# Merge-gate blocks of a prompt attention: eight plain filler products a layer become four seven-product pairs, and the fifth pair follows

## The reference

```
h = RMSNorm(x);  P = h @ w_in
A = NSA(P)      compressed, selected and window softmax attention, sigmoid gates
B = GLA(P)      gated linear attention, per-head RMSNorm, swish output gate
x += (sigmoid(gA) * (A @ w_pa) + sigmoid(gB) * (B @ w_pb)) @ w_out
x += (gelu(conv3(h2 @ w_u)) * (h2 @ w_g)) @ w_down,   h2 = RMSNorm(x)
```

## Time and profile before

| what | value |
|---|---|
| median of 3 runs (lowest, highest) | 2190.35 us (2189.44, 2193.3) |
| profiled execution, its own time | 2181.98 us |
| its span | 2180.2 us |
| mean granted TensorE clock | 0.993 of full speed |
| TensorE / VectorE / ScalarE / GpSimd busy | 98% / 51% / 23% / 27% |
| attention units 1 to 31, first layer | 306 to 462 us |

### The profile page before, as it was taken

One profiled execution on the slowest core, in us unless ns is written; L12 is line 12 of the kernel. 1 busy time (PEld: TensorE's weight loads), 2 busy tenths in 40 slices (PEclk: granted clock), 3 DMA queues, 4 the chain that ended last, 5 costly groups with the idle time before them and its releaser, 6 DMA issues.

```text
span 2180.2 us, 30270 instructions
## 1 busy us (share of the span) xinstructions
PE 2130.5 (98%) x12007; PEld 1708.9 (78%) x12007; DVE 1115.2 (51%) x2318; ACT 511.5 (23%) x1100; POOL 585.5 (27%) x565
## 2 busy tenths in 40 slices
PE   8998999999999999999999989999999999999999
PEld 7786866678887888888887867766788878888887
DVE  5566646654345555543326666466544364555522
ACT  3123124432112222210112231343221212222000
POOL 5140010102322444434331400101032224444332
PEclk9999999999999999999999999999999999999999
DMA  6774531112221322222293736311132222222222
GB/s 167 259 250 167 223 126 39 40 42 100 78 81 59 96 78 78 80 78 92 59 293 115 265 136 247 101 36 24 47 114 81 78 70 85 78 78 91 77 77 74
DMA packets 172303, 237.52 MB, mean 109 GB/s; under 512 B 39551, under 2 KB 151680, under 8 KB 169408
## 3 DMA queue, kind: packets, MB, share of 16 engines
q1 hardware_dynamic: 153320, 133.11, 20.3%
q0 software_dynamic: 18400, 102.36, 12.7%
q10 hardware_dynamic: 444, 0.12, 0.0%
HBM read 222.76 MB, written 21.11 MB: 112 GB/s over the span
## 4 chain that ended last, share of the span: by engine, by line
PE 90%; DVE 5%; DMA 2%; ACT 2%; issue 1%; POOL 0%; DVEq 0%; SPq 0%; ACTq 0%; POOLq 0%
PE PS L948 44%; PE PS L891 18%; PE PS L1077 6%; PE PS L913 5%; PE PS L939 3%; PE PS L1411 2%; PE PS L1328 2%; PE PS L1339 2%; DMA arena<-in_cache_kv_slc_dram,idx 2%; PE PS L442 2%; ACT arena L1621 1%; PE PS L1286 1%; DVE arena L2307 1%; PE PS L1311 1%; DVE arena L1997 1%
## 5 line engine op out<-in xcount | busy, mean ns | idle before, releaser
L948 PE MATMUL PS<-arena,ring 128*128 128x272 f32 x1536 | 376.7, 393 | 0.9 <-DVE xT L1991 0.6
L1621 ACT ACTIVATE arena<-PS 128x272 f32<-128x272 f32 (+11 forms) x438 | 175.6, 425 | 770.1 <-PE PS L948 277.8
L891 PE MATMUL PS<-hT,ring 128*128 128x272 f32 x1408 | 338.9, 400 | 3.1 <-DVE small L2473 1.9
L948 PEld LDWEIGHTS PS<-arena,ring 128*128 128x128 f32 x1536 | 291.5, 190 | 61.5 <-issue 1.7
L891 PEld LDWEIGHTS PS<-hT,ring 128*128 128x128 f32 x1408 | 270.0, 194 | 67.4 <-issue 12.2
L1991 DVE TENSOR_TENSOR arena<-PS,arena 128x272 f32<-128x272 f32 (+4 forms) x222 | 106.6, 489 | 327.2 <-PE PS L948 237.3
L1991 DVE TENSOR_TENSOR xT<-PS,xT 128x272 f32<-128x272 f32 x224 | 98.9, 442 | 252.2 <-PE PS L948 252.0
L948 PE MATMUL PS<-hT,ring 128*128 128x272 f32 x832 | 207.6, 393 | 0.1
L948 PEld LDWEIGHTS PS<-hT,ring 128*128 128x128 f32 x832 | 158.3, 191 | 32.9
L1997 DVE SCALAR_TENSOR_TENSOR arena<-arena,prm 128x32 f32<-128x32 f32 (+1 forms) x176 | 142.6, 810 | 22.1 <-ACT arena L1621 18.2
L948 PE MATMUL PS<-arena,kv_kT 128*128 128x272 f32 x616 | 149.7, 392 | 0.0
(11 more groups left out here) (350 smaller groups left out, 2754.2 us busy)
## 6 DMA issues: line engine op xcount, KB each, us to landing
ring<-in_w_up_dram SPq DMA_DIRECT2D x88, 512.0 KB, 4.6
ring<-in_w_in_dram SPq DMA_DIRECT2D x68, 512.0 KB, 4.8
ring<-in_w_down_dram SPq DMA_DIRECT2D x32, 512.0 KB, 4.5
arena<-in_state_kv_win_dram POOLq DMA_DIRECT2D x4, 2048.0 KB, 8.3
ring<-in_w_out_dram SPq DMA_DIRECT2D x16, 512.0 KB, 4.6
out_dram<-in_state_kv_win_dram POOLq DMA_DIRECT2D x2, 4064.0 KB, 39.9
ring<-in_w_down_dram SPq DMA_DIRECT2D x16, 384.0 KB, 3.8
ring<-in_w_in_dram SPq DMA_DIRECT2D x16, 256.0 KB, 4.6
```

What stands on the lines that cost most here:

```text
L891: mm = pe.matmul(PS[0:m, b + a, 0:HALF], weight(k), rhs(k)[:, HALF * a:HALF * a + HALF], start=(k == 0), stop=(k == nk - 1))
L948: mm = pe.matmul(PS[:, bank, 0:HALF], weight[:, k, :], rhs(k), start=(start and k == 0), stop=(stop and k == kc - 1), skip_group_check=not ...
L1621: return nc.scalar.activation(out, in_, func, **kw)
```

## The change

`ma0` to `ma3` become fillers of seven products each (`side_seven`), after units 9, 15, 21 and 28, in place of eight plain fillers after units 8, 11, 14, 17, 20, 23, 26 and 30. They use one pair of banks: each bank is accumulated on after ScalarE has copied, or VectorE has added, what stood in it. `mb0` becomes a `gate_seven`, with the third and fourth head norm between its second and third product. GpSimd makes the token sums before the attention units instead of in unit 22 (the third in three pieces), changes `hT` in place after `rb11`, and makes the weight sums of `ma0` at once, of `ma1` to `ma3` each after the pair before it, and of `mb0` after the sampled updates. ScalarE and VectorE get the copies and additions; counters and buffers are renumbered.

```diff
-    for j, name in zip((2, 5, 8, 11, 14, 17, 20, 23, 26, 30), ["rb10", "rb11"] + [f"ga{m}" for m in range(KC)]):
+    for j, name in zip((2, 5, 9, 15, 21, 28), ["rb10", "rb11"] + SIDED):
...
-                gp.wait_ge(*S.at(gp, "kd_ready", 1))
+                def weight_sums(name):
...
+                    if n >= EARLY + 2:
+                        gp.wait_ge(*S.filled(gp, last_ticket(SEVENS[n - 2])))
+                    elif 1 <= n < EARLY:
+                        gp.wait_ge(*S.filled(gp, last_ticket(SEVENS[n - 1])))
+                    gp.wait_ge(*w_landed(gp, name))
...
-                gp.tensor_tensor(gsum[2], high[:, :, 0:HALF], gsum[1], ALU.subtract).then_inc(*S.inc(gp, "g_sum"))
+                gp.tensor_tensor(gpair, high[:, 0:2, 0:HALF], gsum[1][:, 0:2, :], ALU.subtract).then_inc(*S.inc(gp, "g_sum"))
+                for k in (2, 3):
+                    gp.tensor_tensor(gsum4[k], high[:, k, 0:HALF], gsum[1][:, k, :], ALU.subtract).then_inc(*S.inc(gp, "g_sum"))
+                weight_sums("ma0")
+                gp.wait_ge(*S.filled(gp, "rb11"))
+                gp.tensor_tensor(low[:, :, HALF:NT], high[:, :, HALF:NT], low[:, :, HALF:NT], ALU.subtract).then_inc(*S.inc(gp, "g_sum"))
+                for name in SIDED[1:]:
+                    weight_sums(name)
...
+                gp.wait_ge(*S.filled(gp, "us3"))
+                weight_sums("mb0")
...
+            def side_seven(name, pool):
...
+                half_product(x, quarter(s, 4, 0, 0), lambda k: hT[:, k, 0:HALF], 4, True, True).then_inc(*S.inc(pe, "side_part"))
+                pe.wait_ge(*S.at(pe, "g_sum", 1))
+                pe.wait_ge(*S.at(pe, "w_sum", 4 * n + 1))
+                half_product(z, new[0], lambda k: gsum[0][:, k, :], 4, True, True).then_inc(*S.inc(pe, "side_part"))
+                pe.wait_ge(*S.at(pe, "side_copied", 3 * i + 1))
...
+                half_product(x, new[1], lambda k: gsum[1][:, k, :], 4, False, True).then_inc(*S.inc(pe, "side_part"))
+                pe.wait_ge(*S.at(pe, "side_copied", 3 * i + 2))
+                pe.wait_ge(*S.at(pe, "w_sum", 4 * n + 4))
+                half_product(z, new[2], lambda k: hT[:, 4 + k, HALF:NT], 4, False, True).then_inc(*S.inc(pe, "side_part"))
+                pe.wait_ge(*S.at(pe, "side_copied", 3 * i + 3))
+                pe.wait_ge(*S.at(pe, "g_sum", 6))
+                half_product(x, quarter(s, 4, 0, 1), lambda k: hT[:, k, HALF:NT], 4, False, True).then_inc(*S.inc(pe, "side_part"))
+                pe.wait_ge(*S.at(pe, "side_met", 3 * i + 1))
+                half_product(z, quarter(s, 4, 1, 0), lambda k: hT[:, 4 + k, 0:HALF], 4, True, True).then_inc(*S.inc(pe, "side_part"))
+                pe.wait_ge(*S.at(pe, "side_met", 3 * i + 2))
+                pe.wait_ge(*S.at(pe, "g_sum", 5))
+                half_product(x, quarter(s, 4, 1, 1), lambda k: gsum4[k], 4, False, True).then_inc(*S.fill(pe, name))
...
-                sb_ = wload("mb0")
-                fm("S", "gb0", sb_, 0)
-                out_norm(2)
-                out_norm(3)
-                fm("S", "gb1", sb_, P)
...
+                gate_seven(0, "S", last_norms)
...
-                    ahead = j + 3 if ("u", j - 1) in SIDE_AT else j + 2
+                    before = SIDE_AT.get(("u", j - 1), ("",))[0]
+                    if before in SIDED_AT:
+                        n, m = SIDED_AT[before], 2 * SIDED_AT[before]
+                        if done < min(j + 2, len(units)):
+                            exps(done)
+                            done += 1
+                        side_take(before, 6 * n + 1, 0, gaT[:, m, 0:HALF])
+                        side_take(before, 6 * n + 2, 1, gaT[:, m + 1, HALF:NT])
+                    ahead = j + 3 if before else j + 2
                     while done < min(ahead, len(units)):
                         exps(done)
                         done += 1
+                    if before in SIDED_AT:
+                        side_take(before, 6 * n + 3, 0, gaT[:, m, HALF:NT])
...
+                        if name in SIDED_AT:
...
+                            dv.wait_ge(*S.at(dv, "side_part", 6 * n + 4))
+                            dv.wait_ge(*S.at(dv, "side_copied", 3 * n + 3))
+                            tt(d0[:, HALF:NT], PS[:, b + 1, 0:HALF], d0[:, HALF:NT], ALU.add).then_inc(*S.inc(dv, "side_met"))
+                            dv.wait_ge(*S.at(dv, "side_part", 6 * n + 5))
+                            tt(d1[:, HALF:NT], PS[:, b, 0:HALF], d1[:, HALF:NT], ALU.add).then_inc(*S.inc(dv, "side_met"))
+                            dv.wait_ge(*S.at(dv, "side_part", 6 * n + 6))
+                            tt(d0[:, 0:HALF], PS[:, b + 1, 0:HALF], d0[:, 0:HALF], ALU.add).then_inc(*S.inc(dv, "side_met"))
+                            dv.wait_ge(*S.at(dv, "side_met", 3 * n + 3))
+                            dv.wait_ge(*S.filled(dv, name))
+                            copy(d1[:, 0:HALF], PS[:, b, 0:HALF]).then_inc(*S.drain(dv, name))
...
+                    if h == 1:
+                        add_seven("mb0", "gb0", "gb1", sB[0], sB[1])
```

More of the change, by code:

```diff
@@ L239, in last_ticket @@
         return f"{kind}{2 * i}"
-    if kind == "mb" and i:
+    if kind == "ma":
+        return name
+    if kind == "mb":
         return f"gb{2 * i}"
@@ L498, in quarter, with weight_parts @@
             return ring[:, slot, 0:2 * kc * WCOLS].rearrange("p (k n) -> p k n", n=WCOLS)[:, kc * lower:kc * lower + kc, P * second:P * second + P]
+        def weight_parts(name, kc):
+            n = SEVEN_AT[name]
+            if n >= EARLY:
+                return [sums[(n - EARLY) % 2][:, i, 0:kc, :] for i in range(3)]
+            return early_sums + [late_sum[n // len(SIDED)]]
         def down_pool(n):
@@ L949, in half_product, with seven_products @@
                 return mm
-            def seven_products(name, pool, first, second, kc, top, low, right, t1, t2, t3, t4, taken, between=None, ready=None):
+            def seven_products(name, pool, first, second, kc, top, low, right, t1, t2, t3, t4, taken, between=None, ready=None, middle=None):
                 n, s = SEVEN_AT[name], wload(name)
-                new = sums[n % 2][:, :, 0:kc, :]
+                new = weight_parts(name, kc)
                 pe.wait_ge(*S.claim(pe, pool, first))
@@ L972, in seven_products @@
                 pe.wait_ge(*S.at(pe, "w_sum", 4 * n + 4))
-                half_product(z, new[:, 2], right, kc, False, True).then_inc(*S.fill(pe, second))
+                half_product(z, new[2], right, kc, False, True).then_inc(*S.fill(pe, second))
                 if between:
@@ L1821, in exps, with side_take @@
                     last.then_inc(*S.inc(act, "ep"))
+                def side_take(name, part, bank, out):
+                    act.wait_ge(*S.at(act, "side_part", part))
+                    run(out, PS[:, S.banks(act, name) + bank, 0:HALF], ACT.Copy).then_inc(*S.inc(act, "side_copied"))
                 def decay_step(step):
@@ L1893, in take_last @@
                     run(out, PS[:, S.banks(act, ticket), 0:HALF], ACT.Copy).then_inc(*S.drain(act, ticket))
-                for m in range(2):
-                    act.wait_ge(*S.filled(act, f"gb{m}"))
-                    b = S.banks(act, f"gb{m}")
-                    run(two(sB[m]), pair2(b), ACT.Sigmoid).then_inc(*S.drain(act, f"gb{m}"))
-                for i in range(1, 4):
+                norm_root(act, run, 0)
+                norm_root(act, run, 1)
+                for i in range(4):
                     c, name = 2 * i, f"mb{i}"
@@ L1904, in _ @@
                     take(name, 0, f"gb{c}", g0[:, 0:HALF])
+                    if i == 0:
+                        norm_root(act, run, 2)
+                        norm_root(act, run, 3)
                     take(name, 1, f"gb{c + 1}", g1[:, HALF:NT])
```

118 lines of the change are left out of this document (65 added, 53 removed).

## The result

The changed kernel takes **2200.71 us** (median of 5 runs, 2197.86 to 2202.30) against 2190.35 for the kernel before on the same chip (2189.44 to 2193.84): a ratio of 1.0038, 95% interval 1.0026 to 1.0051. It is slower by 0.4%, although TensorE now has 40 matmuls of the program fewer to do, 20 a layer. The profile shows 80, since it lists two matmul instructions (and two weight loads) for each of them: x12007 before, x11927 after, and x32 for a plain block of 16. So in the chain, too, x32 is not 16 matmuls with 16 weight loads, as said ahead of the prediction; the prices a block that were read from it do not change. The profiled execution took 2197.86 us, its span 2196.1.

The account below looks back on a forecast made before the run. The prediction took TensorE to bound the kernel (busy 2130.5 of 2180.2 us), with fillers also covering VectorE and ScalarE. Its terms summed to +4.2 us a layer, +8.4 in all, giving a median of 2199 us, range 2184 to 2213.

Parts of the forecast that it names:

- Products, -8.1: Prompt attention: eight fillers of 7.53 us (60.2 a layer) become four long ones of 13.0 (52.1), -8.1 us a layer.
- the long filler stalls inside: Rival, chance 0.10: ScalarE or VectorE late for the long fillers' banks, so seven products cost what eight did; 2215 us.
- Old wait at the token sums, -3.3 and -2.1: Moving GpSimd's token sums away removes TensorE's 3.3 us wait and 2.1 us of low clock a layer.
- New wait at unit 2, +4.6 and +2.1: GpSimd's moved token sums hold VectorE, so unit 2 is turned 4.6 us later, plus 2.1 of clock loss, a layer.
- the lock does not bite: Rival, chance 0.20: VectorE gets its five instructions in before or between GpSimd's sums; 4.6 and 2.1 fall away, 2185 us.
- Units 10 to 15, +7.3 and +1.0: First to second long filler, 20.0 us: TensorE waits 8.5 us against 1.2 before, plus 1.0 for clock, a layer.
- about 8 us of idle: Sign that the forecast is right: about 8 us of idle TensorE between the first and second long filler.
- the short gaps keep the clock low: Rival without its own chance: units 10 to 15 fall to 1.2 GHz, 2 to 3 us a layer more, 2204 us.
- Units 16 to 21, +4.5: Second to third long filler: 20.2 us against 15.7 for the units, as ScalarE's exponentials lose cover; +4.5 us a layer.
- The fifth block, -1.8: Fifth gate block, among the head norms: four matmuls fewer, -1.8 us a layer, with nothing taken for weight sums and additions.
- the table load: ScalarE's step in units 10 to 15: 1.28 us a load taken; the skill's 2.7 would add 2.8 us a layer.
- everything is covered: Rival, chance 0.05: unit 2 is spared and the decay steps find slack, -15.3 us a layer plus little, 2160 us.

Follow-up runs that it names:

- h: f, with GpSimd's weight sums for the later three long fillers held until about 2 us before each; 2167.67 us, ratio 0.9883.
- c: The kernel before, with GpSimd's three token sums held until unit 25 is weighed; 2185.63 us, ratio 0.9971.
- a_sums_covered: The changed kernel, with GpSimd's sums held until a filler runs and its state loads moved behind the first two; 2187.70 us, ratio 0.9978.
- f: d, with VectorE's decay steps moved under the long fillers too and ScalarE's exponentials moved to the third; 2167.01 us, ratio 0.9885.
- b_act_covered: The changed kernel, with ScalarE's two decay steps one unit earlier, under the first and second long filler; 2193.89 us, ratio 1.0011.
- i: h, with the sixth gate block in the other pool's banks; 2164.86 us, ratio 0.9876.
- d: The changed kernel with both the covered GpSimd sums and the covered ScalarE decay steps; 2175.03 us, ratio 0.9927.

## Why the prediction was right

Direction, size and range held: 2199 was forecast, 2200.71 measured, within 2184 to 2213. The mechanism held too, a gain in products paid back by lost cover at unit 2 and between the long fillers. That the number is as close as 1.7 us is in part luck: several terms were off by about 1 us a layer and offset each other, and the stages account for 7.6 of the 10.4 us only. Point by point, per layer of the profiles:

- **Products, -8.1.** The long fillers take 13.03, 13.01, 13.00 and 12.94 us for the 13.0 worked out, so the rival *the long filler stalls inside* is out for this change (in h, with the weight sums pushed late, it does occur: 14.20). The gain is real and was bought back elsewhere: in h, with nearly all the waits gone, the units stage is 150.4 us against 158.0 for c, the kernel before freed of its own wait, 7.6 of the 8.1.
- **Old wait at the token sums, -3.3 and -2.1.** c shows 6.0 and 5.0 us for the two layers, 5.5 on average for the 5.4 of the sum.
- **New wait at unit 2, +4.6 and +2.1.** The wait was 4.54 us in both layers, and the clock cost more than the 2.1: 2.3 and 2.6 us in the filler (9.8 and 10.1 for 7.5) and 0.5 in the two pieces ahead of it (0.69 and 0.70 us for 0.44 each). With the short waits beside it a_sums_covered shows 7.7 and 8.0 us a layer for the 6.7 of the two terms. (The five sums counted end at 306.3 + 7.8 = 314.1 us, the time used for unit 2, and not at the 314.4 written beside them.) The five instructions counted (two biases, the weighting product, two scalings) are the ones that the timeline shows held, one for each sum, and the rival *the lock does not bite* falls with it.
- **Units 10 to 15, +7.3 and +1.0.** The stretch from the first to the second long filler is 19.80 us for 20.0, with the step of ScalarE at the place worked out (its exponentials resume at 371.30, 8.4 us behind the filler, forecast 8.6). The split was off, and the sign "about 8 us of idle" was not met: idle time is 5.6 us by the windows, and the rest a slow clock (TensorE's 14.36 busy us are 11.7 in f). So the rival *the short gaps keep the clock low* was half true inside the stretch: a slow clock behind the waits of 2.55 and 1.40 us brought it to 0.83 over the whole. The filler behind was not slow (13.01), so the term of +1.0 came out at nothing. The length was right because I counted ScalarE and VectorE, not TensorE. b_act_covered shows how little the clock matters there. Windows of this stretch in its first and second layer, in one execution:

```profile
367.61:385.06 17.45, 12.04 (x97) 6.84 (x97) 16.52 (x48) 9.82 (x29) 5.03 (x4) 1.00 0.19 61
1449.33:1466.79 17.46, 13.51 (x98) 7.62 (x97) 16.52 (x48) 9.91 (x29) 5.03 (x4) 0.90 0.20 60
```

  TensorE is busy for 12.04 and 13.51 us, at a clock of 1.00 and 0.90, and the length is the same: a slower TensorE only fills its own waits, while VectorE, busy 16.52 us in both, sets the pace.
- **Units 16 to 21, +4.5.** 20.18 us in the first layer and 19.91 in the second for 20.2 (the pieces written down add to 20.3).
- **The fifth block, -1.8.** This term was mis-sized: the gates stage gives -1.02. I had looked for cover of its weight sums and its additions, and both were covered; the bank was not looked at. The seven products with the two norms take 16.7 us (526.61 to 543.34), as forecast, but the next block's first product claims the bank that the fifth's last product fills, and waits for ScalarE's copy: it starts 0.74 us late and loses nearly 0.1 more, and 1.83 less this 0.8 is the 1.02. In i the stage gets 0.60 and 0.43 us back.
- **What I had at nothing:** the linear stage. It is 1.7 us shorter in one layer of after, by the clock, which is chance for this change (below).

Sum of the terms +8.4 us; the stages show +7.6, the medians +10.4. For the table load I had gone by the row of 1.28 us against the longer figure of the Trainium skill (ScalarE: Activation LUTs, "What ACT_TABLE_LOAD costs"), which adds a drain to a load of that length. The loads of after take 1.28 again, and the next function starts where the load ends (367.58 + 1.28, then 368.88), so no drain shows here, and the stretch came out at the length that this gives.

The rival *everything is covered* had the right number for another kernel. 2160 was what the change would give if nothing waited; f, h and i, which put the waits under the fillers by hand, reach 2165 to 2168.

## What to carry to other kernels

A block of matmuls that stands between dependent steps is paid work and cover at once: taking a seventh off it is a gain only if what it covered is moved with it. Before merging or moving such blocks, list by place what the other engines do under each, and move these steps in the same edit; here the same products are 0.4% slower (after) or 1.15% faster (f_vector_covered) by the place of the other engines' steps. Short sums on GpSimd belong under a stretch in which nobody waits for VectorE, and a bulk operation of VectorE belongs under such a stretch too, not ahead of the reduction that TensorE waits for.

## What the runs showed of the hardware

**The lock holds in both directions.** In f_vector_covered VectorE has a product of two SBUF tensors of 1088 columns (1.28 us alone) beside GpSimd's sums of 512 columns (1.27 us alone). VectorE's timeline, then GpSimd's:

```profile
414.11 2.04 DVE L2065 TENSOR_TENSOR arena<-kbT,arena 128x1088 f32<-128x1088 f32 x1
```

```profile
413.73 1.27 POOL L831 TENSOR_TENSOR arena<-ring 128x512 f32<-128x512 f32 x1 [23.57 <-PE PS L978]
415.08 2.20 POOL L833 TENSOR_TENSOR ring<-ring 128x512 f32<-128x512 f32 x1
```

VectorE starts while GpSimd's first sum runs and is 0.76 us late; GpSimd's second sum starts while that product runs and is 0.93 us late. The rule of the Trainium skill that I weighed (SBUF - State Buffer, "two separate sides": whichever starts first holds the pair of ports for its whole instruction) is borne out here. At unit 2 it cost GpSimd nothing to speak of, as VectorE's instructions there are 0.16 us long: the 0.5 us that the rule would have added is not in the 4.54.

**A slow clock without a wait.** The linear stage of the same work came out at 56.05, 57.7 or 59.35 us over the eleven kernels, and the differences lie between 32 and 44 us into it, where TensorE is busy without a gap in all of them. Over the last 8 us of that the granted clock is 1.00 in the stages of 56.05, 0.79 to 0.81 in those of 57.7, and 0.61 to 0.63 in those of 59.35. What TensorE does from 32 to 36 us is small matmuls on 32 rows and 64 columns of the array; TensorE's timeline of after:

```profile
502.78 3.92 PE L1501 MATMUL PS<-xT,arena 32*64 32x128 f32 x64
```

Windows of the stretch in after and in c_before_late_sums:

```profile
506.57:514.57 8.00, 8.00 (x58) 7.32 (x55) 1.42 (x2) 0.60 (x1) 7.62 (x8) 1.00 0.11 33
```

```profile
498.83:506.83 8.00, 8.00 (x41) 6.74 (x39) 1.43 (x3) 0.00 (x0) 5.75 (x8) 0.62 0.34 106
```

0.62 over the stretch means that part of it runs at the lower of the two levels, 1.2 GHz. Adding 1.83 or 3.67 us of matmuls ahead of the stage changed the outcome, and one execution had both outcomes in its two layers. So it may hang on the moment at which the stage begins; that is not shown, and what decides stays open. In practice up to 6.6 us of a result here, 0.3%, can come from a stage that the edit does not touch: b and c each lost about that much against d and after. An edit of that size should be judged by its stage as well as by its total.
